# A decoder step on one core: 288 prompt tokens' experts gathered instead of 256, 232 columns dense instead of 264, and roots as exp(-ln/2)

## The reference

```python
def rmsnorm(x, g):
    y = xf * lax.rsqrt(jnp.mean(xf * xf, axis=-1, keepdims=True) + EPS)
    return (y * g.astype(F32)).astype(x.dtype)
...
    def block(tb):
        q = (tb @ wq).reshape(P_BLOCK, P_HEADS, 2, P_DKEY // 2)
        s = jnp.einsum('thcd,chkd->thck', q, keys.astype(q.dtype)).astype(F32)
        sv, si = lax.top_k(s, P_TOPK)
        cand = sv[..., 0, :, None] + sv[..., 1, None, :]
        cid = si[..., 0, :, None] * P_NKEYS + si[..., 1, None, :]
        fs, fi = lax.top_k(cand.reshape(P_BLOCK, P_HEADS, P_TOPK * P_TOPK), P_TOPK)
        eid = jnp.take_along_axis(cid.reshape(P_BLOCK, P_HEADS, P_TOPK * P_TOPK), fi, axis=-1)
        g = jax.nn.softmax(fs, axis=-1)
        act = jax.nn.gelu(jnp.einsum('td,thkd->thk', tb, u_tab[eid]).astype(F32), approximate=False)
        w = (g * act).astype(tb.dtype)
        return jnp.einsum('thk,thkd->td', w, v_tab[eid])
```

## Time and profile before

| what | value |
|---|---|
| median of 3 runs | 3930.68 us (3927.41 to 3939.23) |
| the profiled execution | 3938.14 us, its span 3936.5 us |
| busy: PE, PEld, DVE, ACT, POOL | 90%, 74%, 64%, 14%, 20% |
| granted TensorE clock, mean | 0.94 |
| moved by DMA | 1090 MB, mean 277 GB/s |
| by slice of 98 us, GB/s | 93 to 334 in the first 23, 368 to 417 in the last 17 |

### The profile page before, as it was taken

The page is one execution under the profiler, slowest core; times in us unless marked ns, Lnnn a source line. Parts: engine busy times, 40 slices in busy tenths (PEclk is TensorE's granted clock), DMA queues, the critical chain, the costliest instruction groups (busy, mean ns, idle before and its releaser), DMA issues.

```text
span 3936.5 us, 41100 instructions
## 1 busy us (share of the span) xinstructions
PE 3546.1 (90%) x15837; PEld 2905.5 (74%) x15837; DVE 2500.9 (64%) x4048; ACT 535.7 (14%) x1049; POOL 804.8 (20%) x645
## 2 busy tenths in 40 slices
PE   8988887998988887978987799999998999999999
PEld 6765444876777676856776687887887887888887
DVE  4444655534877646657868589666665665666666
ACT  2232222021123322020123100000000000000000
POOL 0000110000011112210000244223323323322233
PEclk9988888987999899988998899999999999999999
DMA  4333545452367656854444799999999999999999
GB/s 168 124 122 123 182 165 182 147 169 93 120 252 257 221 187 231 334 220 150 160 172 182 286 368 369 415 414 409 408 414 376 414 414 397 406 414 417 415 405 379
DMA packets 217893, 1090.49 MB, mean 277 GB/s; under 512 B 23075, under 2 KB 64291, under 8 KB 112099
## 3 DMA queue, kind: packets, MB, share of 16 engines
q0 software_dynamic: 89680, 595.47, 38.5%
q1 hardware_dynamic: 125570, 475.09, 31.9%
q10 hardware_dynamic: 2448, 17.30, 1.1%
HBM read 1051.29 MB, written 36.47 MB: 276 GB/s over the span
## 4 chain that ended last, share of the span: by engine, by line
PE 65%; DVE 18%; DMA 7%; SPq 3%; issue 3%; ACT 3%; POOL 1%; DVEq 0%; ACTq 0%
PE pj L310 21%; PE pst L1943 17%; PE pj L1976 17%; SPq L2073 3%; DVE gs L1887 3%; DMA gs<-in_peer_v,arena 3%; DMA ring<-in_up 2%; PE pst L964 1%; DMA gs<-in_peer_u,arena 1%; DVE arena L561 1%; DVE arena L1040 1%; DVE arena L1041 1%; DVE acc L1895 1%; PE pj L1573 1%; DVE arena L2017 1%
## 5 line engine op out<-in xcount | busy, mean ns | idle before, releaser
L1943 PE MATMUL pst<-hb,ring 128*128 128x264 f32 x4096 | 946.4, 391 | 36.1 <-DMA ring<-in_up 33.2
L1976 PE MATMUL pj<-arena,ring 128*128 128x264 f32 x4096 | 935.5, 388 | 26.9 <-DVE arena L1966 13.1
L1943 PEld LDWEIGHTS pst<-hb,ring 128*128 128x128 f32 x4096 | 787.2, 193 | 176.1 <-DMA ring<-in_up 36.7
L1976 PEld LDWEIGHTS pj<-arena,ring 128*128 128x128 f32 x4096 | 782.7, 191 | 162.6 <-DVE arena L1966 13.3
L1895 DVE SCALAR_TENSOR_TENSOR acc<-gs,arena,acc 128x2048 f32<-128x2048 f32 x256 | 601.6, 2350 | 215.9 <-DMA gs<-in_peer_v,arena 209.8
L1928 POOL DMA_INDIRECT gs<-in_peer_u,arena x256 | 378.1, 1477 | 1545.3 <-DVE arena L1887 1342.8
L1887 DVE CUSTOM_DVE_ANT_0 gs<-gs,hnat 128x2048 f32<-128x2048 f32 x256 | 586.3, 2290 | 123.6 <-DMA gs<-in_peer_u,arena 108.8
L310 PE MATMUL pj<-hb,ring 128*128 128x256 f32 x2048 | 482.5, 392 | 8.9 <-DVE hb L265 7.8
L1928 POOL DMA_INDIRECT gs<-in_peer_v,arena x256 | 346.1, 1352 | 699.2 <-DVE acc L1895 651.9
L310 PE MATMUL pj<-gs,ring 128*128 128x264 f32 x1792 | 457.4, 410 | 7.1 <-DVE gs L265 5.7
L310 PEld LDWEIGHTS pj<-hb,ring 128*128 128x128 f32 x2048 | 396.4, 197 | 73.3 <-issue 15.9
(11 more groups left out here) (418 smaller groups left out, 2690.3 us busy)
## 6 DMA issues: line engine op xcount, KB each, us to landing
ring<-in_w SPq DMA_DIRECT2D x160, 1024.0 KB, 4.8
ring<-in_up SPq DMA_DIRECT2D x128, 1024.0 KB, 9.9
ring<-in_down SPq DMA_DIRECT2D x256, 512.0 KB, 10.7
xb<-in_cache_k POOLq DMA_DIRECT2D x32, 512.0 KB, 5.3
xb<-in_cache_v POOLq DMA_DIRECT2D x32, 512.0 KB, 3.5
gates<-mix ACTq DMA_DIRECT2D x16, 1024.0 KB, 3.9
mix<-gates SPq DMA_DIRECT2D x16, 1024.0 KB, 21.0
arena<-in_state_ssm POOLq DMA_DIRECT2D x8, 512.0 KB, 9.6
```

Source lines behind the costliest of these rows:

```text
L1943: m = pe.matmul(pst[:, j % 2, 0:TD], ring[:, j % 2, c * P:(c + 1) * P], hb[:, c, :], start=(c == 0), stop=(c == DC - 1))
L1976: m = pe.matmul(sums(n), value_tile(n)[:, k * P:(k + 1) * P], wt[:, r % SLOTS * EG + k, :], start=(k == 0), stop=(k == EG - 1))
```

## The change

**288 tokens gathered.** The first 32 tokens of group B leave the dense columns. Each of their 128 experts' rows is gathered with four experts to a DMA: partition 32g+t holds token t and expert 32g+n, so 32 DMAs from each table do for them. `ROWS` goes from 512 to 576. The tokens are turned once by 16 transposes (`extra_turn_*`), kept in DRAM, copied four times into `hnat`; their choices go to `xeid` and `xgw` by eight small DMAs (`extra_choices`), and the four partial sums of a token are added by a matmul of each chunk with `xsum` (`extra_sums_pe`), near the end. The dense part has TD = 232 columns, 14 instead of 16 gate batches, and 58 instead of 66 chunks of gates.

**Rows earlier.** 181 rows are ahead of the dense loop: 7 instead of 4 for a head, 6 instead of 3 for a pair, 24 as before in the output projection, 8 instead of 4 in the cross attention, 12 instead of 4 in its output, 16 instead of 4 in the sorts and 17 instead of 8 in the gates. The last four steps have none.

**One-hots.** VectorE makes the high one with its weight (`highs_dve`, four instructions of 128 columns), ScalarE the low one as relu(1-|x|) (`lows_act`). 24 of the 58 chunks now run between the sorts.

**Roots.** `Ln` with a scale and a bias, then `Exp` of minus a half, both on ScalarE and from one table (`LN_EXP`). The number of table loads in ScalarE's order is 44, it was 101.

**Order in attention and pairs.** In the attention TensorE's steps stand one or more quarters later against the tiles. In the pairs of group A the four products of the samples are spread through the pair, sums and maxima of the samples have moved to another bank (`pst`), and the transposed output goes to the next pair.

```diff
 def norm_act(act, k, cols):
+    act.wait_ge(s_sqsum, DC // 2 + k)
+    hold(act, s_root, k)
+    act.activation(nrt[:, 0:cols], pst[:, 0, 0:cols], ACT.Ln, bias=eps, scale=1.0 / D).then_inc(s_var, 1)
     act.wait_ge(s_var, k + 1)
-    act.activation(nrt[:, 0:cols], nrt[:, 0:cols], ACT.Sqrt).then_inc(s_root, 1)
+    act.activation(nrstd[:, 0:cols], nrt[:, 0:cols], ACT.Exp, scale=-0.5).then_inc(s_root, 1)
...
 def norm_dve(dve, o, k, src, dst, gain, cols):
-    dve.wait_ge(s_sqsum, DC // 2 + k)
-    dve.tensor_scalar(nrt[:, 0:cols], pst[:, 0, 0:cols], 1.0 / D, EPS, ALU.mult, ALU.add).then_inc(s_var, 1)
     dve.wait_ge(s_root, k + 1)
-    o.step(dve.reciprocal(nrstd[:, 0:cols], nrt[:, 0:cols]))
...
     quarter(0, 0)
-    if do_att:
-        values()
-        scores(0)
+    attend(values)
     quarter(0, 1)
+    attend(scores, 0)
     quarter(0, 2)
-    if do_att:
-        scores(1)
     quarter(0, 3)
-    if do_att:
-        transposes(0)
+    attend(scores, 1)
...
+    XT = 32
+    XG, GD, TD = P // XT, GT - XT, TA - XT
+    NBATCH = GD // 16
...
-    ROWS = 4 * P
-    R_ATT, R_SSD, R_CROSS, R_WO = 4, 3, 1, 4
+    ROWS = 4 * P + 2 * XT
+    R_ATT, R_SSD, R_CROSS, R_WO = (1, 1, 1, 1, 2, 1), (2, 1, 2, 1), 2, 12
     R_OUT = tuple(1 + n % 2 for n in range(DC))
-    R_SEL = tuple(hd % 2 for hd in range(PH))
-    R_GATE = tuple(int(q % 8 == 7) for q in range(NQ))
+    R_SEL, R_GATE = 2, 1
...
 def weight_of(st):
+    if st >= STEPS - 4:
+        return 0.0
     return 0.5 if st < EG or st >= STEPS - 2 * EG else 1.0
...
     for c in range(DC):
-        m = pe.matmul(pst[:, j % 2, 0:TD], ring[:, j % 2, c * P:(c + 1) * P], hb[:, c, :],
+        m = pe.matmul(pst[:, j % 2, 0:TD], ring[:, j % 2, c * P:(c + 1) * P], hb[:, c, XT:TA],
...
+def highs_dve(dve, q):
...
+    for i in range(4):
+        t = 4 * q + i
+        dve.tensor_scalar(hots[:, q % 2 * 2 + 1, i * P:(i + 1) * P], co("iota"), flat[:, 0, t:t + 1],
+                          flat[:, 2, t:t + 1], ALU.is_equal, ALU.mult).then_inc(s_hot, 1)
+def lows_act(act, q):
...
+    for i in range(4):
+        t = 4 * q + i
+        act.activation(low[:, i * P:(i + 1) * P], co("iota"), ACT.Abs, bias=flat[:, 1, t:t + 1],
+                       scale=-1.0).then_inc(s_low, 1)
+    act.wait_ge(s_low, 5 * q + 4)
+    act.activation(low, low, ACT.Relu, bias=1.0, scale=-1.0).then_inc(s_low, 1)
...
+def extra_sums_pe(pe):
+    pe.wait_ge(s_gl, NU)
+    pe.wait_ge(s_used, ROWS)
+    for c in range(DC):
+        m = pe.matmul(pst[:, 0, c * XT:(c + 1) * XT], acc[:, c * P:(c + 1) * P], xsum, start=True, stop=True)
...
-FLAT = {2: 0, 14: 1}
-CHUNKS = {j: range(8 * (j - 15), min(8 * (j - 14), NQ)) for j in range(15, EARLY)}
+FLAT = {2: 0, 18: 1}
+def chunks(j):
+    def upto(k):
+        if k < 18:
+            return NQ_HALF * max(k - 3, 0) // 14
+        return NQ_HALF + (NQ - NQ_HALF) * (k - 18) // 5
+    return range(upto(j - 1), upto(j))
```

More of the change, by code:

```diff
@@ L978, in pairs_pe, with sample_rows @@
                 m.then_inc(s_y, 1)
-            quarter(1, 2)
-            quarter(1, 3)
-            if ssd and gi == 0:
-                pe.wait_ge(s_opvc, s + 1)
+            def sample_rows():
+                hold(pe, s_opvc, s)
+                pe.wait_ge(s_qm, s + 1)
+                pe.wait_ge(s_rowc, 2 * g + 2)
+                for b in range(2):
+                    m = pe.matmul(pst[:, b, :], ones[0:TS, :], qmask[0:TS, b * 512:(b + 1) * 512], start=True, stop=True)
+                m.then_inc(s_qrow, 1)
@@ new lines, in pairs_pe @@
+            quarter(0, 1)
+            if ssd:
+                broadcast()
+            quarter(0, 2)
+            if ssd:
+                turned()
+            quarter(0, 3)
+            quarter(1, 0)
+            if ssd:
+                states()
+            quarter(1, 1)
+            if sampled:
+                sample_max()
+            quarter(1, 2)
+            if sampled:
+                sample_shift()
+            if ssd:
+                outputs()
+            if sampled:
+                sample_sums()
@@ L1103, in pairs_dve @@
[L1103 to L1117 removed]
+                dve.wait_ge(s_gape, 2 * S + 2)
@@ new lines, in decayed, with carry @@
+                o.last(dve.tensor_tensor(gap[:, :, :], gap[:, :, :], gflat[:, None, g * GT:(g + 1) * GT]
+                                         .broadcast_to([P, 2, GT]), ALU.mult))
+            def carry(dst, src, b, done):
+                for e in range(2):
+                    r = slice(e * SP_, (e + 1) * SP_)
+                    m = dve.scalar_tensor_tensor(out=dst[:, r], in0=src[:, r],
+                                                 scalar=dec[:, e, (b + 1) * P - 1:(b + 1) * P],
+                                                 in1=pov[:, b * P + e * SP_:b * P + (e + 1) * SP_],
+                                                 op0=ALU.mult, op1=ALU.add)
+                    if e and done:
+                        m.then_inc(s_hst, 1)
+                    elif e:
+                        o.step(m)
+                    else:
+                        o.last(m)
```

546 lines of the change are left out of this document (318 added, 228 removed).

## The result

| | before | after |
|---|---|---|
| median | 3932.18 us (3927.41 to 3939.23, 4 runs) | 3877.11 us (3856.68 to 3886.95, 4 runs) |
| ratio, 95% interval | | 0.9852 (0.9806 to 0.9898) |
| the profiled execution | 3938.14 us, span 3936.5 | 3856.68 us, span 3855.0 |
| granted TensorE clock | 0.940 | 0.918 |
| table loads in the trace | 101 | 44 |

The kernel became faster by 55 us, not by the 158 of the forecast, and 3877 lies outside the range of 3705 to 3840. The direction was right, the size was wrong. One more thing is new: executions of the changed kernel spread over 30 us, those of the kernel before over 12, and the one with the trace was the fastest of its four. Two traces compared give a gain of 81 us; the medians give 55.

What follows compares the result with a forecast made beforehand. TensorE waiting at a low clock bounds the front; TensorE and the DMA together bound the dense loop. Gains 72 (group A), 1 (group B), 29 (early up tiles), 56 (loop) sum to 158 us: 3773 us, range 3705 to 3840.

Steps and rivals of the forecast that it cites:

- Columns: Dense loop, TensorE: with 232 columns instead of 264, 32 matmul instructions take 6.3 us instead of 7.12.
- The DMA sets the step: Dense loop: the DMA needs 13.98 us a step, above TensorE's 12.6; 0.26 us less, 24 us over 92 steps.
- rival (c): Dense loop: the DMA can carry more, so a step falls to TensorE's 12.6 us; whole 3646 us; chance 0.04.
- The 20 us of recovered stalls: Dense loop: of 33 us that broken places cost the DMA, 20 come back, since TensorE's slack repays late tiles.
- Rival (a): Dense loop: SP's hangs at the small gate load swallow its 56 us gain; whole 3829 us; chance 0.15.
- The rest of the loop's forecast: Dense loop: 24 us over 92 steps, 6 in the 16 last, 3 in the first eight, 3 in steps 8 to 18.
- Pairs of group A: Group A's pairs: VectorE work moved behind the transposes' input gives 36 us a pair against 39.5, 28 us less.
- Attention of group A: Group A's attention: the new order hides waits for exponentials, 2.3 us for each of 8 heads, 7 for the last: 25.
- the sum of 72: All of group A, with first norm, ends and other norms: 72 us less, bounds 20 and 130.
- Group B: Group B, carrying 60 of the 81 extra early rows: 1 us less in sum, bounds 35 less and 60 more.
- rival (d): Group B: gathered rows land late, past 12 us, and starve VectorE; whole 3980 us, slower; chance 0.04.
- Early up tiles: Stage before the dense loop: 291 us instead of 320, 29 less, with ScalarE the bound of the last 34 chunks.

Runs made afterwards that it cites:

- the run with the fill: Changed kernel plus 20 extra unread TensorE products of 128 columns a pair in group A, ahead of TensorE's waits for VectorE: 3851.55 us, ratio 0.979.

## Why the prediction was wrong

**Columns: right.** Tiles take 6.27 us (6.3 forecast).

**The DMA sets the step: right, but the step was sized short.** With half of the loop's rows gone every step is 12.5 us. The rate was right too (undisturbed 410 to 418; 415 in 3400 to 3600), and rival (c) is out. Over the last 88 steps with an up tile a step took 14.75 us before, 14.39 and 14.58 in the two traces after, and with the gate loads on ScalarE's queue 14.46 before and 14.32 after: 0.14 us gained by the change, where 0.26 was forecast. One cause is in the sum itself. It took the bytes of a step from 14.24 us at 414 GB/s, 5.90 MB; its own count of rows, tiles and gates is 5.95, which needs 14.38 us at that rate. By this count the DMA was over TensorE's 14.24 before the change already.

**The 20 us of recovered stalls: wrong.** This term said that slack in TensorE would repay late tiles. It can't where the DMA is the cap: time that the queue loses is lost. The two runs on ScalarE's queue price the term: the hang cost 23 us before and 32 after, so 9 us more were lost in place of 20 gained. The gain of the loop was 35 and 11 us in the two traces, not 56. Rival (a), that the hangs swallow the loop's gain, had the right mechanism and a chance of 0.15, but its 56 us were too many: the hang's growth took 9. The rest of the loop's forecast, 36 us without the 20, came short too. With the hang out of both kernels the loop to the last down tile went from 1688 to 1664.4 us, 23 less: some 12 in the 88 steps, 11 ahead of them, none behind the last up tile (133 us in both), where 6 were forecast. At the 409 GB/s of before the 18.7 MB fewer would have been 46 us; the rate over the whole loop fell to 404, and no run says why.

**Pairs of group A: wrong, 28 us for 0.** Three sizes in one term failed. First, 39.5 us a pair before: the starts of value products give 38.7. Second, 36 after: VectorE's row was taken as all of its 27 us and the turn to the next pair as 2, where it is 20.0 and 10.3, so that part of VectorE's work lies beside TensorE and most of the turn doesn't; with the 7 us of value products the sum is 37.3 instead of 36. The gain of an ordinary pair is then 1.4 us, not 3.5. Third, the slow clock was taken as unchanged; it stayed the same in length (116 us of 355 in both traces) but moved: in the pair where the second half of the heads begins, time at half clock rose from 20 to 34 us, and that pair took 6 us more (2 more in the four traces with 24 us at half clock). What the ordinary pairs and the end of the stage gained, some 9 us, this pair and the first took back. The share of the clock in this is read from where the half-clock time lies in the two traces; that the clock costs some 2 us in an ordinary pair is what the run with the fill showed, and the rest of its price stays open.

**Attention of group A: right** (27.5 for 25). The smaller terms of group A brought 10 for 19. No run shows the 8 us that the sum of 72 has for the memory attention; the two traces gave 4.9 (177.1 to 172.2), at a clock of 0.81 and 0.83.

**Group B: right.** Sum 4 us for 1, with each part within 4 us. A row landed in 9.5 us (median between 1043 and 1850 us; 8.1 before), under the 12 at which rival (d) begins. VectorE waited 6.5 us for the up rows in all.

**Early up tiles: 4 us for 29.** The last 34 chunks are as forecast: ScalarE at 2.6 us each (2.95 forecast), 125 us for 120. What failed is the part ahead of them: 158 us forecast, 176 measured. The sum counted VectorE's work and not its wait for a free pair of buffers, which comes with the product two chunks earlier, and this stands behind up tiles on TensorE. The run with rows between the chunks gives 10 of these 18 us back; the other 8 are not shown apart. The remaining 7 us of the miss are those chunks with their up tiles (125 for 120) and the gates' way through memory (15 for 13).

**The median.** The forecast took off the 7.5 us by which the profiled run of before stood above its median. After, the profiled run stood 20 below. The two together are 28 us that no term could have seen, except by asking whether a loop that hangs on a full queue will spread.

**Range and chances.** The range was too narrow since the three large terms had no room downward together. All three leaned on the same assumption, that a shorter cost on one engine reaches the end.

## What to carry over

Before a gain is booked for a stage, put its row together from the chain of one period: start to start of the same instruction, and each stretch in between by engine. A mean of stage starts and an engine's busy time hide both the turn and the waits for buffers. Where a loop is bound by the DMA, a strided load with many small pieces belongs on a queue on which nothing urgent stands behind it, and work that costs bytes in the loop belongs beside an engine that waits elsewhere: here a row moved ahead cost 0.4 to 1.1 us and saved 2.1 to 2.5. To see what a change gains without a fault that both kernels have, take the fault out of both: without the hang the changed loop is 53 us shorter than that of the kernel before as it stands, but only 23 us shorter than that of the kernel before without the hang.

## What was unexpected of the hardware

A DMA of 1792 pieces of 512 B issues in 0.43 us on SP, but the next DMA on the same queue, the small load or an up tile, is held for up to 31 us while the DMA is full (31.2 in the run with the old pairs, a median of 19.9 in the first trace of the changed kernel). On ScalarE's queue, where no other load of the loop stands, the small load takes 0.35 us and the strided one behind it 0.45, in all 14. The same hang costs little where the DMA has room: with half of the rows gone its median is 3.4 us, and no step was lost to it.
